# Attention values ahead of the steps beside them on TensorE's queue, in a streaming encoder layer

## The reference, cut to what matters

```
hn   = norm(x) * (1 + sc1) + sh1
proj = hn @ w_in                      # u, q, k, v, 512 columns each
pool = per-group map of (trailing means of u, minus u), windows 2, 4, 8, 16
attn = stick-breaking attention, 8 heads of 64:
       z = q k / 8;  a[t,s] = sigmoid(z[t,s]) * prod over s<j<t of (1 - sigmoid(z[t,j]));  attn = a v
mix  = concat(pool, attn) @ w_out
x1   = layer_norm(ALPHA * x + (1 + g1) * mix)
hn2  = norm(x1) * (1 + sc2) + sh2
ff   = mixture of 16 experts on hn2: top group, top 2 of its 4 experts
y    = layer_norm(ALPHA * x1 + (1 + g2) * ff)
```

## Time and profile before

| | us |
|---|---|
| median of 3 runs | 863.57 |
| lowest, highest | 863.53, 867.05 |
| profiled execution | 863.53 |
| its span | 861.8 |
| TensorE matmul busy | 792.0 (92%) |
| VectorE busy | 597.8 (69%) |
| ScalarE busy | 349.7 (41%) |
| GpSimd busy | 314.2 (36%) |

### The profile page before, as it was taken

How to read it: one execution, slowest core, us unless ns; L and a number is a source line. 1 busy time by engine, 2 the same in 40 slices (tenths; PEclk the granted TensorE clock), 3 DMA queues, 4 the chain that set the end, 5 groups by cost and what they waited for, 6 DMA issues and landing times. The chain is left out here.

```text
span 861.8 us, 13448 instructions
## 1 busy us (share of the span) xinstructions
PE 792.0 (92%) x4805; PEld 625.4 (73%) x4806; DVE 597.8 (69%) x685; ACT 349.7 (41%) x645; POOL 314.2 (36%) x259
## 2 busy tenths in 40 slices
PE   3899999999978899999999995599999999999894
PEld 2689999999945566766767784378888888888641
DVE  6679679852079965875777566998557998563097
ACT  3811110111156763444444435544544444444144
POOL 3000799960000001000000001257665897663156
PEclk9999999999999999999999996699999999999897
DMA  8956544630073501321102037798779998889594
GB/s 322 397 175 204 163 152 132 200 98 2 1 257 144 144 17 50 100 72 38 62 26 74 25 122 265 279 327 278 272 253 334 401 384 289 278 306 345 175 355 157
DMA packets 77362, 165.32 MB, mean 192 GB/s; under 512 B 7397, under 2 KB 32517, under 8 KB 75266
## 3 DMA queue, kind: packets, MB, share of 16 engines
q1 hardware_dynamic: 68402, 132.15, 44.2%
q0 software_dynamic: 7760, 28.31, 9.3%
q10 hardware_dynamic: 1152, 4.19, 1.4%
HBM read 132.57 MB, written 32.08 MB: 191 GB/s over the span
## 5 line engine op out<-in xcount | busy, mean ns | idle before, releaser
L2101 PE MATMUL psum<-we_hi,x_parts 128*128 x384 | 137.5, 403 | 1.4 <-DVE we_lo L1724 1.1
L1724 DVE TENSOR_TENSOR we_lo<-we_raw,we_hi 128x2048 fp32r<-128x2048 f32 x48 | 116.1, 2422 | 1.5
L1723 DVE CAST we_hi<-we_raw 128x2048 fp32r<-128x2048 f32 x44 | 60.7, 1379 | 47.9 <-DMA we_raw<-in_w_down_dram 24.5
L449 PE MATMUL psum<-hn_hi,w_hi 128*128 128x364 f32 (+1 forms) x384 | 90.7, 331 | 1.3 <-issue 0.7
L449 PE MATMUL psum<-hn_lo,w_hi 128*128 128x364 f32 (+1 forms) x384 | 90.1, 329 | 0.0
L449 PE MATMUL psum<-hn_hi,w_lo 128*128 128x364 f32 (+1 forms) x384 | 89.9, 328 | 0.0
L2101 PEld LDWEIGHTS psum<-we_hi,x_parts 128*128 128x128 f32 x384 | 72.1, 188 | 16.5 <-issue 2.3
L1040 PE MATMUL psum<-wo_hi,mixin 128*128 128x512 f32 (+1 forms) x256 | 83.2, 396 | 0.6 <-DVE logits L1367 0.6
L2101 PE MATMUL psum<-we_lo,x_parts 128*128 x192 | 75.2, 392 | 0.0
L633 DVE SCALAR_TENSOR_TENSOR proj<-wm,cT,proj 128x2048 f32<-128x2048 f32 x28 | 72.6, 2638 | 0.1
L449 PEld LDWEIGHTS psum<-hn_hi,w_hi 128*128 128x128 f32 x384 | 67.0, 189 | 5.7 <-issue 4.8
(11 more groups left out here) (334 smaller groups left out, 1587.3 us busy)
## 6 DMA issues: line engine op xcount, KB each, us to landing
we_raw<-in_w_up_dram SPq DMA_DIRECT2D x32, 1024.0 KB, 8.4
wm<-in_w_mod_dram SPq DMA_DIRECT2D x16, 1024.0 KB, 5.3
we_raw<-in_w_down_dram SPq DMA_DIRECT2D x16, 1024.0 KB, 6.6
w_raw<-in_w_in_dram SPq DMA_DIRECT2D x16, 512.0 KB, 6.2
we_raw<-ff_d SPq DMA_DIRECT2D x12, 512.0 KB, 8.3
proj<-in_x_prompt_dram SPq DMA_DIRECT2D x4, 1024.0 KB, 8.1
sc_room<-in_w_mod_dram SPq DMA_DIRECT2D x4, 1024.0 KB, 14.0
proj<-in_w_mod_dram SPq DMA_DIRECT2D x2, 2048.0 KB, 12.2
```

The lines of the kernel that those rows point to most:

```text
L449: mm = pe.matmul(psum[:, 3 * slot + c, 0:n], w[:, slot, k, :], hn[:, k, t0:t0 + n], start=(k == 0 and w is w_hi and hn is hn_hi), stop=(k ...
L1723: then(dve.tensor_copy(we_hi[:, a:b], raw))
L1724: dve.tensor_tensor(we_lo[:, a:b], raw, we_hi[:, a:b].bitcast(F32), ALU.subtract).then_inc(ready, 1)
L2101: mm = pe.matmul(psum[:, bank, :], x[:, s, k, :], w[:, bass.ds(at + k * 2 * DE, 2 * DE)], start=(k == 0 and x is x_hi and w is we_hi), sto ...
```

## The change

In the loop of TensorE the values of unit u-3 are issued behind the turn of unit u-2, ahead of the steps beside of iteration u, in every iteration from 3 on. Before, they came behind the steps beside in iterations 3 to 55, and ahead of them only from 56 on.

```diff
--- before.py
+++ after.py
@@ -1082,7 +1082,7 @@
                     scores(u)
                 if 0 <= u - LAG < nu:
                     turn(u - LAG)
-                if u >= nu:
+                if u > LAG:
                     values(u - LAG - 1)
                 if u < 2:
                     for n in ((4, 5, 6), (7, 8))[u]:
@@ -1106,8 +1106,6 @@
                         turn_k(n)
                     else:
                         router(n)
-                if LAG < u < nu:
-                    values(u - LAG - 1)
 
         @block.scalar
         def _(act):
```

## The result

The change makes the kernel slower: 868.63 us, the median of 13 runs, against 865.13 us of the kernel before in 13 runs beside them; ratio 1.0053, with a 95% interval of 1.0040 to 1.0066, or 3.5 to 5.7 us (the two medians alone give 3.5 us, the lower end). The profiled execution has a span of 865.4 us against 861.8. Half of the working in the prediction came true: the waits moved nearly as it said. The time went where it had put nothing, into TensorE's busy time. (The profiled execution of the changed kernel had a mean granted clock of 0.974, while all 30 runs of it on record have 0.966 on the mean; that of the kernel before had 0.968, as its runs do.

The account below looks back on a forecast made before the run. VectorE sets the pace in the first 39 us of attention, TensorE later, with mutual waits from 383 to 450. +2.5 +1.6 +0.4 −5.06 −1.5 = −2.1 us from 863.57 gives 861.5 us; 8 in 10 between 857.8 and 866.5.

Parts of the forecast that it names:

- So all rests on waits.: Whole change: matmul blocks and steps beside only change places, so only waits were expected to change the time.
- (a): 246 to 321 us: steps beside no longer cover waits, TensorE 2.5 us late by unit 28; bounds none and 5.
- if VectorE's idle time takes it up: Bound for 246 to 321 us: no loss, if VectorE's 1.5 idle us there absorb the lateness.
- 2 to 3 us later than 321.03: Sign of being right: at iteration 28, first product of line 1040, TensorE is this much later than before.
- The last landmark: Sign of being right: at the scores of 450.45 TensorE is earlier by about 3 us.
- (b): 338 to 386 us, after second half projections: cover lost, 1.6 us; after 450 us 0.4; bounds of both 0 and 4.
- (c): 383 to 450 us: four TensorE waits go, before M0:3, T0:1, T2:1 and T0:2, gaining 5.06 us; bounds 3.9 and 5.06.
- (d): 446 to 448 us: half clock behind the 1.90 us wait goes with it, gaining 1.5 us; bounds 1.5 gained, 0 or below.
- second rival: New waits in 262 to 386 us make the clock fall, 1.5 us each: 864.5 to 869.0 us, slower; chance 0.15.
- Of the rivals, the clock: The second rival: clock falls in the new waits of 262 to 386 us make the kernel slower; chance 0.15.
- short idling between groups of matmuls: Skill's rule that such idling while PSUM banks are cycled makes the clock swing; the trace bore it out for 2 waits.

Follow-up runs that it names:

- e8_first: Values ahead of the steps beside only in iterations 3 to 27, order of before from 28 on; 869.91 us against 864.73 of the kernel before, ratio 1.0055.
- e4_before_turn: Kernel before with values of unit u-3 issued before the transposes, between scores and turn, in iterations 3 to 55; 879.24 against 864.47 us, ratio 1.0170.
- e2_m_early: Kernel before with values ahead of the steps beside only in the 14 iterations with a half projection; 864.09 against 864.47 us, ratio 0.9986.
- isolated measure: Kernel before plus 12 small matmuls ahead of each of 18 half projections, two tile forms alternating against grouped; 912.30 against 897.47 us.

## Why the prediction was wrong

It forecast 861.5 us and a gain of 2.1; measured was a loss of 3.5 to 5.7. Point by point, in its own steps:

- *"No instruction is added or removed ... So all rests on waits."* This step failed. The same instructions in another order kept TensorE busy for 5.1 us more, at nearly the same half clock (5.8 and 6.6 us), by 32 more changes of tile form. Forecast and measured change of the span are 5.7 us apart (−2.1 and +3.6): +5.1 are this term, +1.5 the clock gain that was not there in the stage, −0.7 the waits, which came out better than forecast (−1.24 against −0.56), and −0.2 lies outside the stage. It could have been seen before: weight loads idle for 0.17 us or more in front of scores, turn and values, and not in front of the half projection that follows the turn. I had read block lengths as constants that could be exchanged; the length of a block depends on its neighbour.
- *(a) Cover lost, 2.5 us.* The mechanism was right, the size was not: +0.71 us of idle time (e8_first: +0.67). The steps of the walk added up latenesses, while the waits that stood in this stretch already took up part: the one of 1.07 us for TV:8 went, and 1.06 and 1.93 us became 1.50 and 2.21. The case "if VectorE's idle time takes it up", kept as a bound, was nearer. That TensorE is nonetheless 4.6 us late at unit 28 looks like the prediction's landmark ("2 to 3 us later than 321.03") overfulfilled; it is the form and the clock, 2.5 and 1.4 us. The last landmark failed with it: the scores of 450.45 were to come 3 us earlier and stand at 452.75, 2.3 us later.
- *(b) 1.6 and 0.4 us.* Right in place (waits in iterations 31, 33, 35, 39, 53 and 55), somewhat larger: 2.27 and 0.83.
- *(c) 5.06 us of waits go.* Right to the hundredth: 5.05.
- *(d) The clock, −1.5 us.* The fall behind 444 us went, worth 1.1 (0.41 × 2.7, by the window) to 1.5 (by the lengthened matmuls of the prediction), but one stands at 285: nothing in the sum. It looks like the second rival, true once, but kernels with the order of before fell there too, so that its cause stays open. What failed here is the step from one profile to a rule: which waits are followed by a fall changes from one profiled execution to the next, and the mean clock of the changed kernel's 30 runs goes from 0.957 to 0.974.

Of the rivals, the clock was the one that ended on the right side, and that was luck, for its reason carries little of the time: in the stage the two profiled executions have nearly the same half clock, 5.8 and 6.6 us. e4_before_turn may show it at work: where the values wait 19.9 us the granted clock of the first window is 0.86, and half clock costs 10.8 us there against 1.3 before. One profile doesn't settle it, since e2_m_early came to 0.88 there with no new wait; but the mean clock of the five runs of e4_before_turn is 0.960 against 0.968 in 23 runs of the kernel before. So what the prediction took from the Trainium skill on short idling between groups of matmuls agrees with e4_before_turn, as far as its runs go, and hardly bears on the change itself.

The Trainium skill, page "TensorE: Matmul & The Clock Gate", section "Step-by-step: what each phase is for", says that TensorE pulls weight loads ahead of matmuls under way when the row groups don't conflict or when they go to the background buffer. The trace agrees for neighbours of one form (the load at 339.40, 0.28 us before the transposes end) and shows a bound of it: in the kernels before and after, at nearly every change of form between scores, turn, values and the 128*128 steps, the load came together with its own matmul, 0.07 us before the other block's end and no earlier. What in the array makes it so no run here shows.

## What to carry to other kernels

Moving a block on TensorE's queue costs or gains not only waits: count how often neighbouring matmuls change the form of their tile, at some 0.15 us for each here, and compare busy time between the same two points of the program, for idle time doesn't show it. Move a block only in the iterations in which a wait is won: three of 46 moves carried the whole gain (−7.4 us), and the others together took it back and more. And don't expect a wait to bring a fall of the clock, or its going to spare one, from a single profile.

## What was not expected of the hardware

A change of tile form on TensorE takes 0.14 us in the isolated measure (14.8 us for 108, good to 4 us), with no idle time in the row of the matmuls. Half clock cost 0.41 us per us in this mix of small blocks: the same instructions in the same order were busy 68.62 us at 0.98 and 75.58 us at 0.88. And the clock fell at different places in kernels whose order is the same up to there.
